# Even attention of a fused two-block kernel: stack copies placed earlier in the transfer queue, value products made for two duos at a time behind the scores

## What is computed

```
mod_x = silu(c) @ w_mod[l] + b_mod[l]          # six column blocks per layer, also for the context
hx = rms_norm(x) * (1 + sc_x) + sh_x           # hc likewise
px, pc = hx @ w_in_even, hc @ w_in_even        # q k v ga, and bb cb ub gb (the slim chunks and gc)
# differential attention: 8 heads, two maps of 32 features each
s = einsum('bqhmd,bkhmd->bhmqk', q, k) * A_QK**-0.5
p = softmax(s);  a = p[:, :, 0] - lam * p[:, :, 1]
o = einsum('bhqk,bkhd->bqhd', a, v)            # x attends to 768 keys, the context to its own 256
y = b * conv3(c * u)                           # short convolution of the slim chunks
x = x + g_x * rms_norm(concat(o', y') @ w_out[0]);  ctx likewise
```

## Time and profile before

| | |
|---|---|
| median of 3 executions | 1315.1 us (1314.51 to 1316.66) |
| the profiled execution | 1319.82 us, its span 1317.9 us |
| granted PE clock over the span, 1.00 = full | 0.981 |
| PE busy / PEld busy | 1246.1 us / 999.3 us |
| DVE / ACT / POOL busy | 675.4 / 632.7 / 463.3 us |
| the even stage (feeds, scores, values) | 635.6 to 877.3 us of the span |

### The profile page before, as it was taken

One profiled execution on the slowest core, in us unless ns is written; L12 is line 12 of the kernel. 1 busy time (PEld: TensorE's weight loads), 2 busy tenths in 40 slices (PEclk: granted clock), 3 DMA queues, 4 the chain that ended last, 5 costly groups with the idle time before them and its releaser, 6 DMA issues. The chain is left out here.

```text
span 1317.9 us, 19569 instructions
## 1 busy us (share of the span) xinstructions
PE 1246.1 (95%) x7148; PEld 999.3 (76%) x7148; DVE 675.4 (51%) x1293; ACT 632.7 (48%) x1355; POOL 463.3 (35%) x360
## 2 busy tenths in 40 slices
PE   7999999999999999899598989999999999999997
PEld 6877777776788788888476767788878788777785
DVE  4676966655315245547173637551834701555353
ACT  7544327654523366623264646552546422655533
POOL 5544434221444455512132323331452323222351
PEclk9999999999999999999798989999999999999999
DMA  6322541101322523501325341221234232221442
GB/s 230 134 72 70 187 160 65 65 33 49 128 97 95 193 96 106 197 1 65 113 94 182 116 168 59 93 75 65 96 112 146 85 115 86 67 94 65 161 133 91
DMA packets 28429, 140.33 MB, mean 106 GB/s; under 512 B 4304, under 2 KB 5712, under 8 KB 15728
## 3 DMA queue, kind: packets, MB, share of 16 engines
q1 hardware_dynamic: 21584, 117.72, 25.5%
q10 hardware_dynamic: 6752, 21.35, 4.9%
HBM read 122.74 MB, written 6.29 MB: 98 GB/s over the span
## 5 line engine op out<-in xcount | busy, mean ns | idle before, releaser
L1255 POOL TENSOR_TENSOR w_low<-w_raw,w_high 128x512 fp32r<-128x512 f32 x256 | 350.5, 1381 | 653.0 <-ACT w_high L1436 652.4
L1436 ACT CAST w_high<-w_raw 128x512 fp32r<-128x512 f32 x256 | 153.9, 621 | 258.5 <-PE psum L660 171.7
L660 PE MATMUL psum<-x_high,w_high 128*128 128x512 f32 x528 | 219.2, 415 | 3.7 <-DVE e_conv L2614 1.0
L660 PE MATMUL psum<-x_high,w_low 128*128 128x512 f32 x528 | 206.6, 391 | 0.0
L660 PE MATMUL psum<-x_low,w_high 128*128 128x512 f32 x528 | 206.2, 391 | 0.0
L660 PEld LDWEIGHTS psum<-x_high,w_high 128*128 128x128 f32 x528 | 99.7, 189 | 32.8 <-issue 10.1
L660 PEld LDWEIGHTS psum<-x_high,w_low 128*128 128x128 f32 x528 | 99.1, 188 | 21.6
L660 PEld LDWEIGHTS psum<-x_low,w_high 128*128 128x128 f32 x528 | 99.6, 189 | 16.6 <-issue 1.0
L2550 DVE TENSOR_REDUCE small<-psum 128x1 f32<-128x768 f32 (+1 forms) x96 | 70.0, 771 | 72.1 <-PE psum L1040 72.1
L660 PE MATMUL psum<-w_high,x_high 128*128 128x512 f32 x224 | 88.4, 395 | 0.9 <-POOL w_low L1255 0.6
L660 PE MATMUL psum<-w_high,x_low 128*128 128x512 f32 x224 | 87.3, 390 | 0.0
(11 more groups left out here) (484 smaller groups left out, 2862.0 us busy)
## 6 DMA issues: line engine op xcount, KB each, us to landing
w_raw<-stream SPq DMA_DIRECT2D x98, 1024.0 KB, 4.9
x_kept<-arena ACTq DMA_DIRECT2D x8, 512.0 KB, 3.7
arena<-x_kept ACTq DMA_DIRECT2D x8, 512.0 KB, 5.6
arena<-bias ACTq DMA_DIRECT2D x8, 512.0 KB, 3.9
q_masked<-e_q_high SPq DMA_DIRECT2D x24, 96.0 KB, 2.5
arena<-x SPq DMA_DIRECT2D x4, 512.0 KB, 5.2
arena<-x ACTq DMA_DIRECT2D x4, 512.0 KB, 5.0
arena<-ctx ACTq DMA_DIRECT2D x4, 512.0 KB, 4.4
```

What stands on the lines that cost most here:

```text
L660: mm = pe.matmul(o, l, r, start=(first and n == 0 and kind != "fc"), stop=(last and n == len(passes) - 1))
L1255: pool.tensor_tensor(PLACE[u][1], RAW[:, g % 2, u % 4, :], PLACE[u][0].bitcast(F32), ALU.subtract).then_inc(w_lo, 1)
L1436: act.copy(PLACE[u][0], RAW[:, g % 2, u % 4, :]).then_inc(w_hi, 1)
```

## The change

It does seven things: (1) SP issues the stack copies at other places of the stream. (2) `values_even` runs at every fourth step for two duos, into 256 columns of bank 5, and directly behind `score_even` instead of behind the first transposes. (3) `FEED_E` is (3,2), (3,2), (2,2), (1,1) pieces instead of (2,1), (2,1), (2,2), (3,3). (4) Mods stand one step later (3, 11, 19, 35, 43 instead of 2, 10, ..., 42), slot 3 has none, and mod (1,3) becomes a guest of `eo0` behind its units 1 and 4, its row turned after the first tile of `eo1`. (5) `INDEX_SUMS` goes by groups of four. (6) Gate `ga` is multiplied one top-k round earlier. (7) ACT no longer splits `n_k`'s first two units between the two normalizations of the context.

```diff
+GUEST_AT = {"eo0": (1, 4)}
-LATE_HOSTS = ("n_k", "ud")
-EVEN_MODS = [m for m in MODS if m not in MODS[:4] + MODS[10:]]
+LATE_HOSTS = ("eo0", "n_k", "ud")
+EVEN_MODS = dict(zip((0, 1, 2, 4, 5), MODS[4:9]))
...
-        INDEX_SUMS = [6 * pr + n for pr in range(HEADS // 2) for n in (0, 2, 1, 3, 4, 5)]
+        INDEX_SUMS = [first + n for first in range(0, len(INDEX), 4) for n in (0, 2, 1, 3)]
...
-        FEED_E = ((2, 1), (2, 1), (2, 2), (3, 3))
+        FEED_E = ((3, 2), (3, 2), (2, 2), (1, 1))
-        MOD_AFTER = {GRANULE_STEPS * j + 2: mod for j, mod in enumerate(EVEN_MODS)}
+        MOD_AFTER = {GRANULE_STEPS * j + 3: mod for j, mod in EVEN_MODS.items()}
...
             def values_even(d):
                 pr, n = EVEN[2 * d][1], keys_of(2 * d) // P
-                for hh in range(2):
-                    for c in parts_of(2 * d):
-                        consumed(pe, ("e", "T", 2 * d + hh, c))
...
                 acc = open_bank(key, 5)
-                for kt in range(n):
+                for duo in (d - 1, d):
                     for hh in range(2):
-                        head = 2 * pr + hh
-                        mm = pe.matmul(acc[64 * hh:64 * hh + 64, 0:P], E_V[:, kt, 64 * head:64 * head + 64],
-                                       E_PT[:, 2 * (d % 2) + hh, P * kt:P * kt + P], start=kt == 0, stop=kt == n - 1)
+                        for c in parts_of(2 * duo):
+                            consumed(pe, ("e", "T", 2 * duo + hh, c))
+                    own = slice(P * (duo % 2), P * (duo % 2) + P)
+                    for kt in range(n):
+                        for hh in range(2):
+                            head = 2 * pr + hh
+                            mm = pe.matmul(acc[64 * hh:64 * hh + 64, own], E_V[:, kt, 64 * head:64 * head + 64],
+                                           E_PT[:, 2 * (duo % 2) + hh, P * kt:P * kt + P], start=kt == 0, stop=kt == n - 1)
                 fills_bank(mm, key)
...
             for s in range(n):
                 score_even(s)
+                if s >= 7 and s % 4 == 3:
+                    values_even((s - 5) // 2)
                 if s >= 3:
                     turn_even(s - 3, 0)
-                if s >= 5 and s % 2:
-                    values_even((s - 5) // 2)
                 feed("e", pieces, FEED_E[s % 4][0])
...
-            by_tiles("eo1", mixed, gives_back=False)
+            by_tiles("eo1", mixed, lambda t: turn_due(), gives_back=False)
...
-                if g >= granule_of(UNITS["cb_1"][-1]):
+                if g > granule_of(UNITS["cb_0"][-1]):
                     while made < len(STACK_STEPS) and STACK_STEPS[made] < freed_in(GRANULES[g - 2]):
...
             def turned_even(s, c):
                 d, hh = s // 2, s % 2
                 if d >= 2:
-                    filled(act, ("e", "O", d - 2))
+                    filled(act, ("e", "O", d - 2 | 1))
...
-                if s >= 5 and s % 2:
+                if s >= 7 and s % 4 == 3:
                     values_even((s - 5) // 2)
...
             rms("eo_c", LT, lambda t: E_O[:, ST + t, :], context_out, M_JUNK, c=ST)
-            high(UNITS["n_k"][1])
             rms("x3_c", LT, lambda t: E_O[:, ST + t, :], context_summed, M_JUNK, c=ST, each=True)
...
-                if n == 8:
+                if n == 7:
                     gated("ga", GA)
```

More of the change, by code:

```diff
@@ L66 @@
 HOSTS = ("ga", "gb", "vb", "mb0")
-LATE_HOSTS = ("n_k", "ud")
-EVEN_MODS = [m for m in MODS if m not in MODS[:4] + MODS[10:]]
-GUEST = {host: mod for host, mod in zip(HOSTS + LATE_HOSTS, MODS[:4] + MODS[10:])}
+LATE_HOSTS = ("eo0", "n_k", "ud")
+EVEN_MODS = dict(zip((0, 1, 2, 4, 5), MODS[4:9]))
+GUEST = {host: mod for host, mod in zip(HOSTS + LATE_HOSTS, MODS[:4] + MODS[9:])}
 UNITS = {}
@@ L84 @@
     _j, _rest = divmod(4 * _b - UNITS[SLIM[0]][0], 4)
-    if 0 <= _j < len(EVEN_MODS):
+    if _j in EVEN_MODS:
         GRANULES += [("m", EVEN_MODS[_j], half) for half in range(2)]
@@ L771, in gemm @@
                     unit(chunk, k, x, c, part)
-                    if chunk in GUEST and k in (1, 5):
+                    if chunk in GUEST and k in GUEST_AT.get(chunk, (1, 5)):
                         modulate(*GUEST[chunk], int(k > 1))
@@ L1090, in _ @@
             turn_even(n - 2, 0)
-            values_even(n // 2 - 2)
             unit("gc", 2, X, C)
@@ L1374, in freed_in @@
                     return split_in(4 * granule[1] + 3)
-                return min([s for s, mod in MOD_AFTER.items() if mod == granule[1]], default=len(EVEN))
+                return min([s + 1 for s, mod in MOD_AFTER.items() if mod == granule[1]], default=len(EVEN))
             for g in range(N_GRANULES):
-                if g >= granule_of(UNITS["cb_1"][-1]):
+                if g > granule_of(UNITS["cb_0"][-1]):
                     while made < len(STACK_STEPS) and STACK_STEPS[made] < freed_in(GRANULES[g - 2]):
@@ L1574, in _ @@
                 w = P * (t + 1)
-                if n % 6 == 0 and pr + 1 < HEADS // 2:
-                    prep_i(pr + 1)
+                if n % 6 == 0 and n // 6 + 1 < HEADS // 2:
+                    prep_i(n // 6 + 1)
                 if n >= 3:
@@ L1838, in values_even @@
                 x, pr, t, _ = EVEN[2 * d]
-                key, c = ("e", "O", d), P * t if x else S + P * t
+                key, c = ("e", "O", d), P * (t - 1) if x else S + P * (t - 1)
                 ps = filled(act, key)
-                frees(act.copy(E_Q[:, pr, c:c + P], ps[:, 0:P]), key)
+                frees(act.copy(E_Q[:, pr, c:c + 2 * P], ps[:, 0:2 * P]), key)
             def fed_even(s):
@@ L1930, in _ @@
             mixed_out(0, range(ST))
+            guest_rows(GUEST["eo0"])
             def e_ready(t):
@@ L2299, in gated @@
                     frees(dve.tensor_tensor(g[:, j, :], g[:, j, :], BANK[fills[(c, j)][0]][:, :], ALU.mult), (c, j))
[L2301 to L2304, removed]
             def modulation(layer, parts, rows=None):
@@ L2326, in modulation @@
                         consumed(dve, ("modT", layer, i))
-                    scale_up(layer)
+                    a, b = COL[f"npre{layer}"]
+                    link(dve.scalar_tensor_tensor(MC[:, layer, 8:16, :], MC[:, layer, 8:16, :], 1.0,
+                                                  COLS[:, a:b].unsqueeze(2).broadcast_to((P, 8, 2)), ALU.add, ALU.mult))
             link(dve.tensor_scalar(A_MASK[:, 0:P], square("causal"), -1.0, None, ALU.mult))
@@ L2637, in _ @@
             low_mixed([XL[:, j, :] for j in range(4)] + ctx_of(CL), [XH[:, j, :] for j in range(4)] + ctx_of(CH), values, 6)
-            for i in range(4):
+            for i in range(3):
                 consumed(dve, ("modT", 1, i))
-            shifts = COLS[:, COL["bmod1"][0]:COL["bmod1"][0] + 16].unsqueeze(2).broadcast_to((P, 16, 2))
-            link(dve.tensor_tensor(MC[:, 1, :, :], MC[:, 1, :, :], shifts, ALU.add))
-            scale_up(1)
+            biases = COLS[:, COL["bmod1"][0]:COL["bmod1"][0] + 12].unsqueeze(2).broadcast_to((P, 12, 2))
+            link(dve.tensor_tensor(MC[:, 1, 0:12, :], MC[:, 1, 0:12, :], biases, ALU.add))
+            modulation(1, (3,))
             dve.wait_ge(sig("row0"), 4)
```

10 lines of the change are left out of this document (5 added, 5 removed).

## The result

The changed kernel measured 1309.44 us (median of seven executions, 1306.9 to 1312.37) against 1317.19 for the kernel before in the same runs (1314.51 to 1319.37). The ratio is 0.9943, with a 95% interval of 0.9926 to 0.9959: faster by 0.6%, some 7.5 us, where I had forecast 16.7. The forecast of the time itself, 1298.4, was 11.0 too low: 9.0 because the change gave less, and 2.1 because the kernel before measured 1317.19 here and not 1315.1.

What follows compares the result with a forecast made beforehand. PE, busy 95% of the span, was taken as the bound, losing time mainly in the even stage. Stage -14.5, eo1 +3.3, index -2.9 and n_k -2.6 sum to -16.7 us: from 1315.1 to 1298.4, range 1288 to 1310.

Steps and rivals of the forecast that it cites:

- The copies: Even stage: stack copies are issued before PE needs them, so waits of 13.0, 2.2 and 5.05 us go.
- The waits: Even stage: the changed values, feeds and mods bring PE new waits of 20.7 us in sum.
- eo0 and eo1: The mod costs the same in eo0, but eo1 waits for POOL's split units: +3.3 us, bounds 0 and +6.
- Index: Index sums by groups of four remove two waits of 1.46 us: -2.9 us.
- n_k: Context normalizations: DVE's sums end 1.5 us earlier, a 1.6 us clock loss may go: -2.6 us, bounds 0 and -3.7.
- the sum of the stage, -14.5: Even stage: loses 27.5 us instead of 42, with ends of -30 and +8.
- The stream: Even stage: granules 52 to 54 are issued 2 to 5 us later, but none is needed within 5 us of landing.
- The clock: Even stage: five of seven new waits of 1.3 us or more drop the clock, 1.6 us each, 8.0 in all.
- The base: Whole kernel: the profiled execution, 1319.8 us, is 4.7 above the median; -16.7 was applied to both.
- ScalarE's queue as the bound: Steps with two duos: next exponentials also wait for ACT's first copy, 4.4 us a step, kernel at 1318; chance 0.07.
- A clock that falls at every new place: Even stage: 19 places at 1.6 us, 30.4 instead of 8.0, gives 1321, with half the surplus 1310; chance 0.13.
- That the copies don't come early: Even stage: copies wait for something later or the stream pays; 19 of 42 us stay, 1317; chance 0.04.

Runs made afterwards that it cites:

- e4: The changed kernel measured once more, as it is: 1308.86 us, ratio 0.9940 to the kernel before.
- e6: The changed kernel with values of one duo at every second step again and the new feed table kept: 1310.22 us, ratio 0.9932.
- e5: The changed kernel with the old feed table, values still of two duos: 1289.07 us, ratio 0.9779.
- e13: The kernel before with early stack copies (1291.18 us with these alone) plus index sums by groups of four: 1286.95 us, ratio 0.9772.
- e14: The kernel before with early stack copies (1291.18 us with these alone), n_k's units not split between the context's normalizations: 1288.56 us, ratio 0.9794.
- e7: The changed kernel with ACT's copy of the first transposes put behind exponentials and values' copy at steps with two duos: 1308.34 us, ratio 0.9926.
- e15: The changed kernel with ACT's splits of steps 6 and 30 left to steps 7 and 31: 1311.77 us, ratio 0.9962.

## Why the prediction was right and wrong

**Right.** The copies: first score right behind e_v, 13.2 us there, the 5.05 and the 2.25 gone. The 5.85 went with the mod. The waits, in size and place: I had 20.7 us from step 6 on, the profiles show 23.7 and, in e4, 21.9; without those that my list hadn't (next paragraphs) 19.0 and 18.6. Before the mods stand 1.46 and 2.14 where I had 2.15 and 3.1, before the scores of steps 8 and 32 2.7 where I had 1.9. Their cause was right only in part: I hung the mods' waits on the values of two duos, but e6 has 6.9 us of them without these and e5 has 2.0 with them, so it is the few pieces in front of the mods that count. eo0 and eo1: from 909.70 to 1036.27 the stretch is 3.35 us longer; less the mod's 1.9, and with the 1.7 that the context's wait lost put back, 3.1 against my 3.3. Index: -1.95 and -4.92 at the first place of the table, -4.2 in e13, for my -2.9. n_k: -2.6 in e14, for -2.6; that this agrees to the digit is luck, since my own two terms, 1.5 and 1.6, make 3.1, and e14's interval of some 3 us to either side can't tell the two apart. The rule of the Trainium skill (SBUF, Who interferes with whom) on a DVE instruction with two SBUF inputs beside GpSimd is borne out by these rows, by the 4.34 against 2.48 and by the 1.65 against 0.75, as far as the two disturb each other; whether one stands still until the other ends, the rows don't tell. I let it touch one term only, and did not look for it at steps 7 and 31, where the feeds moved the convolution onto POOL's low parts: 2.7 us of wait instead of my 1.9.

**The step that failed is the sum of the stage, -14.5.** Worked out from the table, behind the first place and without the mod that moved, it was -11.8 in the profiled execution and -7.5 in e4. Three sizes were off in it:

- *The end of the stage was left out.* Behind the double values of step 47 come waits that no step of my list had: 0.47 and 1.28 for ACT's copies of transposes and 1.34 for DVE's product in gc, 3.1 in all. In e4 the last of them isn't there; a stretch at half speed from 862 on stands in its place.

```profile
860.42 0.63 PE L1051 MATMUL psum<-squares_sb,arena 128*128 128x128 f32 x4 [1.28 <-ACT arena L1839]
...
865.86 0.38 PE L651 MATMUL psum<-ctx_high,w_high 128*128 128x256 f32 x1 [1.34 <-DVE e_conv L2586]
```

- *The stream.* I said that no granule is needed within 5 us of its landing. In step 36 of the profiled execution ACT waited 6.14 us for one behind a late mod, with ACT's copy of the transposes queued behind the cast, and PE waited 2.94 (1.56 in e4):

```profile
805.02 0.62 ACT L1440 CAST w_high<-w_raw 128x512 fp32r<-128x512 f32 x1 [6.14 <-DMA w_raw<-stream]
```

- *The clock.* I took 8.0 us for five stretches. The profiled execution had two, of 3.5 us each, so 3.5 lost. e4 had six: 0.95 over its 235.4 us, 24 us at half speed, so 12 lost. Behind the same wait of 1.46 before the mod of step 11 the mod took 1.92 in one execution (686.20, above) and 3.32 in the other:

```profile
684.11 3.32 PE L748 MATMUL psum<-w_raw,mod_x 128*32 128x512 f32 x16 [1.46 <-ACT arena L1845]
```

So a wait of that length may or may not drop the clock, and the count is no property of the kernel.

**The base was wrong too.** I took the profiled execution's surplus of 4.7 us over the median as a constant to be carried over. It wasn't: with its clock of 0.981 against 0.983 to 0.986 in most runs, it held, as an estimate (0.002 to 0.005 of 1318), some 3 to 7 us more of clock loss. That this lay in the even stage, where my sum then removed it, is likely and not shown: of its own loss, 0.019 of 1318 or 25 us, 19 were there (0.08 of 241.7), but no other execution of that kernel left a trace. e4, whose profile and median agree within 0.6, is 11.5 below that execution and 7.9 below the median. The 3 us to the median, and 5.2 that e4 is short of my sum, make up nearly all of the 8.8 by which the change fell short of it.

**Rivals.** ScalarE's queue as the bound, at the steps with two duos: e5 keeps these steps and ACT's order and is 20 us faster, so they alone don't make the cost. e7 only shows that another order doesn't help; PE still waits for ACT there. A clock that falls at every new place: two stretches in one execution and six in the other, not 19. That the copies don't come early: out.

**What I had not asked.** I set what the stage lost before against what it would lose after, and never priced parts 2 to 4 alone against a stage with early copies. The rows held it: 42 us less the 13.0, 2.2, 5.05, 5.85 and their clock left a stage that loses, as an estimate, some ten, and my own list of new waits came to 27.5. The finding of this case, that the copies are worth 26 us and the new feeds cost 20, stood, roughly, in those two numbers.

Open: how much of the table's cost is the convolution ahead of the maxima and how much the missing pieces; why the clock falls behind a wait in one execution and not in the other; and how wait and clock share the cost over more than one execution of each kernel.

## What to carry over

When a change has parts that don't need each other, price each against the stage as the others leave it; a sum near the right size can hide a term that eats the gain. A piece of work moved one step earlier moves what it triggers (here a convolution on DVE, closed by the last feed) ahead of something else: follow the trigger, and look at what POOL does at the new place. Don't carry a profiled execution's surplus over the median into a forecast that removes the loss which made it.

## What the chip showed that I had not expected

- DVE's operations with two SBUF inputs took 1.65 us instead of 0.75 (128x511) and 2.17 instead of 1.24 (128x1024) beside POOL's low parts, and 0.75 in the mean of all eight 128x511 ones in e15, where the four that had POOL beside them (steps 7 and 31) had it no more. In e4 the mean of the eight is 1.20.
- A wait of 0.31 us before a unit of eo1 goes with more than its figure: units behind such waits start 1.24 us apart (971.07, 972.31), where unhindered ones start 0.68 apart. The timeline's idle time leaves out what a matmul's modelled end covers. POOL makes these units' low parts at 1.25 each (four in 5.01 from 970.88 on), so it is its pace that PE keeps.
